# Where a norm's gain is applied: on the split weights, or on the transposed rows

## The chip, the cores and the metric

One NeuronCore of a Trainium2 chip runs the whole program in one launch. The metric is the device time of that launch in microseconds (us). The engines are TensorE (PE; PEld is its weight load), VectorE (DVE), ScalarE (ACT), GpSimd (POOL) and SyncE (SP), which issues the weights' DMAs.

## What is computed

Two transformer blocks over 256 tokens of width 1024, in float32. The first has one layer (moving-block attention and retention side by side, cross attention to a memory of 256 rows, a gated feed-forward of width 2816). The second has two layers, one with sparse attention and a short convolution, one with latent attention, each followed by a squared-ReLU feed-forward of width 4096. Every projection reads normalised rows:

```python
def _rms_norm(x, gain):
    xf = x.astype(jnp.float32)
    xf = xf * lax.rsqrt(jnp.mean(xf * xf, axis=-1, keepdims=True) + NORM_EPS)
    return xf.astype(x.dtype) * gain
...
        hn = _rms_norm(x, norm_mix_pre[layer])
...
        x = x + _rms_norm(mix, norm_mix_post[layer])
        hn = _rms_norm(x, norm_ffn_pre[layer])
        x = x + _rms_norm(_squared_relu_mlp(hn, mlp_w1[layer], mlp_w2[layer]), norm_ffn_post[layer])
```

The root of the mean square is one number a token; the gain is one number a feature, that is, one a row of the weight matrix.

## The kernel before

**Products.** The 256 tokens are two tiles (t = 0, 1) of 128 rows. A product of float32 precision is made of three float32r products (`products`, L1325): rows high x weights high, rows high x weights low, rows low x weights high. So both operands are split: high is the value rounded to float32r, low is the value minus high.

**Weights.** They come as 178 units of up to 128 x 2048 (`UNITS`, from `SCHEDULE`), by SyncE into the four slots of `w_raw`. For each unit ACT writes `w_hi` (`split`, L568) and DVE `w_lo` (`split`, L917 without a gain, L919 with one), four slots each; ACT waits until TensorE has used the slot, DVE waits until ACT has done the whole unit, TensorE waits for DVE. A unit is a triple (columns, pieces, gain column): a unit of 2048 columns holds one, two or four blocks of 128 features, and a gained unit is split in that many pieces, since the gain is a column [128, 1] of `gcol` that differs from block to block. Units without a norm in front are one piece.

**Rows.** The residual stream x is turned by TensorE in blocks of 128 x 128, four to a PSUM bank (banks 4 to 7). ACT writes a bank to `hT_hi` (`high_banks`, L587), DVE writes `hT_lo` (`low_banks`, L934), each as one instruction of 128 x 512; DVE's frees the bank, and TensorE waits for that before it reads the tile. A tile is two banks. `gT_hi`, `gT_lo` hold the memory's rows. The token's root is applied to the product when it leaves PSUM.

**The passage between two layers** (`boundary`, `boundary_after`) is written out by hand, the same on both engines. On ACT: square of tile 0 of the product, split of a unit, the high parts of tile 0 of x, square of that tile, split, square of tile 1 of the product, split, the high parts of tile 1, square. On DVE: tile 0 added to the stream (L992, L994), split, low parts of tile 0, split, tile 1 added, low parts of tile 1, split. GpSimd computes each root between the square and the addition (L462, L463). TensorE turns tile 0 before the last unit of the product's tile 1, and tile 1 beside the first product of the next layer. After mlp0 the product's rows are latents, 640 columns, split as five blocks a tile (one bank of four blocks and one of a single block). At the start the rows of x are split on ACT before the first units, and the memory's four banks are split after the third projection group.

Of the kernel before, what the change touches and what calls it, by code (L numbers as in the profile page):

```python
# [49 lines left out]
def gained(gain, count, kcs, size):  # L50

    return [(size, kcs, PRE[gain] + TURNED * j * kcs) for j in range(count)]


def plain_units(count, size=2048):
    return [(size, 1, None)] * count


def hidden_units(gain, chunks, down):
# [13 lines left out]
            ("ukv", [(2048, 2, PRE["ranks"] + 3 * TURNED)] * 2), ("odd_out", plain_units(4)),  # L73
# [28 lines left out]
def block_kernel(nc, A, out):  # L102

    with ExitStack() as ctx:
# [447 lines left out]
        def _(act):  # L552
# [38 lines left out]
            def high_rows(tile, *tiles):  # L591

                for t in tiles or range(TT):
                    high_banks(2, lambda i: (tile[:, 4 * i:4 * i + 4, t * P:(t + 1) * P], 4))
# [55 lines left out]
            def boundary(units):  # L650
# [8 lines left out]
                high_rows(hT_hi, 0)  # L659
# [5 lines left out]
                high_rows(hT_hi, 1)  # L665
                stream_square(1)

            def boundary_after(m):
# [6 lines left out]
                high_rows(hT_hi, 0)  # L675
# [5 lines left out]
                high_rows(hT_hi, 1)  # L681
# [79 lines left out]
            high_rows(hT_hi, 0)  # L761
            act.wait_ge(gcol_ready, len(PRE_ROWS))
            split_to(0)
            high_rows(hT_hi, 1)
# [38 lines left out]
            boundary(4)  # L803
# [6 lines left out]
            boundary(4)  # L810
            mlp(ffn)
            boundary_after(ffn)
# [37 lines left out]
            boundary(4)  # L850
            mlp(mlps[0])
            boundary_after(mlps[0])
# [6 lines left out]
            for t in range(TT):  # L859
# [5 lines left out]
                high_banks(2, lambda i: (hT_hi[:, 4 * i:4 + i, t * P:(t + 1) * P], 4 - 3 * i))  # L865
# [27 lines left out]
            boundary(4)  # L893
# [8 lines left out]
        def _(dve):  # L902
# [35 lines left out]
            def low_rows(hi, lo, tiles=range(TT)):  # L938
                for t in tiles:
                    low_banks(2, lambda i: (hi[:, 4 * i:4 * i + 4, t * P:(t + 1) * P], lo[:, 4 * i:4 * i + 4, t * P:(t + 1) * P], 4))  # L940
# [55 lines left out]
            def boundary(b, units, last=True):  # L996
# [7 lines left out]
                low_rows(hT_hi, hT_lo, [0])  # L1004
# [803 lines left out]
```

## Time and profile before

| what | us |
|---|---|
| median of three runs | 1137.89 (1135.34 to 1138.71) |
| profiled execution, its own time | 1135.04 |
| span of that execution, first to last instruction | 1133.2 |
| TensorE busy (matmul) | 1059.2, 93% of the span |
| DVE busy | 657.8, 58% |
| ACT busy | 563.5, 50% |
| GpSimd busy | 91.6, 8% |
| mean granted clock of TensorE | 0.981 of 2.4 GHz |

Some 2 us of the time lie outside the span. Busy times are sums over one engine's instructions; matmuls are pipelined, so their durations overlap. Times in a timeline are from the start of the span, a duration stands behind them, and in brackets is how long the engine sat idle before and what ended that.

### The profile page before, as it was taken

The numbers are of one execution on the slowest core, as the hardware profiler recorded it, in microseconds if no ns is written. First come the engines' busy times: TensorE is split into PE (matmuls) and PEld (weight loads), VectorE is DVE, ScalarE is ACT, GpSimd is POOL, SyncE is SP. The second block draws the span as 40 slices with busy tenths as digits, with TensorE's granted clock in tenths as the row PEclk, the third lists the DMA queues.
The fourth block names the chain that finished last, engine by engine and source line by source line (L and its number), as shares of the span: only waits on it lengthen the run. The fifth ranks groups of instructions, "written<-read, shape, count | busy, mean of one in ns | idle before, by whom it ended". The sixth has DMA issues, their size and how long they took to land.

```text
span 1133.2 us, 13827 instructions
## 1 busy us (share of the span) xinstructions
PE 1059.2 (93%) x5080; PEld 879.3 (78%) x5080; DVE 657.8 (58%) x1010; ACT 563.5 (50%) x855; POOL 91.6 (8%) x123
## 2 busy tenths in 40 slices
PE   6898999998999999899988899999988998999997
PEld 5687778777888888788767688888886776888886
DVE  5457565347456455647696755555564866555553
ACT  5466365336455454545444555444445645554441
POOL 1010010001000000201840100000040001000000
PEclk9899999999999999889999999999999999999999
DMA  8632145314354555454322644454244225445520
GB/s 331 255 150 112 38 171 214 155 75 144 137 218 152 190 214 185 142 186 149 140 84 75 222 168 172 180 204 160 77 136 161 76 75 223 153 182 208 187 85 37
DMA packets 28589, 176.29 MB, mean 156 GB/s; under 512 B 3440, under 2 KB 3824, under 8 KB 10112
## 3 DMA queue, kind: packets, MB, share of 16 engines
q1 hardware_dynamic: 26496, 170.08, 40.8%
q0 software_dynamic: 1296, 5.24, 1.3%
q8 instruction: 29, 0.48, 0.2%
q10 hardware_dynamic: 752, 0.36, 0.1%
q14 instruction: 16, 0.13, 0.0%
HBM read 174.62 MB, written 1.05 MB: 155 GB/s over the span
## 4 chain that ended last, share of the span: by engine, by line
PE 77%; DVE 9%; ACT 5%; issue 3%; POOL 2%; POOLq 0%; ACTq 0%; DVEq 0%
PE PS L1325 68%; PE PS L1388 3%; DVE w_lo L919 3%; ACT w_hi L568 2%; PE PS L1440 2%; PE PS L1518 2%; PE PS L1423 2%; ACT work L637 1%; DVE w_lo L917 1%; DVE h L992 1%; DVE x L994 1%; DVE work L1031 1%; POOL h L486 1%; PE PS L1431 1%; ACT hT_hi L587 1%
## 5 line engine op out<-in xcount | busy, mean ns | idle before, releaser
L919 DVE SCALAR_TENSOR_TENSOR w_lo<-w_raw,gcol,w_hi 128x512 fp32r<-128x512 f32 (+4 forms) x322 | 269.4, 894 | 218.2 <-ACT w_hi L568 218.0
L1325 PE MATMUL PS<-w_hi,hT_hi 128*128 128x512 f32 (+3 forms) x904 | 322.9, 398 | 33.0 <-DVE w_lo L919 14.7
L1325 PE MATMUL PS<-w_hi,hT_lo 128*128 128x512 f32 (+3 forms) x904 | 315.2, 390 | 0.0
L1325 PE MATMUL PS<-w_lo,hT_hi 128*128 128x512 f32 (+3 forms) x904 | 315.1, 390 | 0.0
L568 ACT ACTIVATE w_hi<-w_raw,gcol 128x512 fp32r<-128x512 f32 (+4 forms) x322 | 243.5, 824 | 99.0 <-PE PS L1325 98.8
L1325 PEld LDWEIGHTS PS<-w_hi,hT_hi 128*128 128x128 f32 x904 | 170.7, 193 | 72.4 <-issue 18.7
L1325 PEld LDWEIGHTS PS<-w_hi,hT_lo 128*128 128x128 f32 x904 | 172.4, 192 | 34.2
L1325 PEld LDWEIGHTS PS<-w_lo,hT_hi 128*128 128x128 f32 x904 | 172.7, 192 | 33.1
L917 DVE TENSOR_TENSOR w_lo<-w_raw,w_hi 128x2048 fp32r<-128x2048 f32 (+1 forms) x70 | 135.8, 1954 | 98.2 <-ACT w_hi L568 98.1
L568 ACT ACTIVATE w_hi<-w_raw 128x2048 fp32r<-128x2048 f32 (+1 forms) x70 | 114.8, 1645 | 113.1 <-PE PS L1325 113.1
L1325 PE MATMUL PS<-w_hi,gT_hi 128*128 128x512 f32 x408 | 126.8, 392 | 1.2 <-DVE w_lo L919 1.2
L1325 PE MATMUL PS<-w_hi,gT_lo 128*128 128x512 f32 x408 | 126.2, 391 | 0.0
L1325 PE MATMUL PS<-w_lo,gT_hi 128*128 128x512 f32 x408 | 126.1, 390 | 0.0
L1325 PEld LDWEIGHTS PS<-w_lo,gT_hi 128*128 128x128 f32 x408 | 76.9, 188 | 16.2
L1325 PEld LDWEIGHTS PS<-w_hi,gT_lo 128*128 128x128 f32 x408 | 76.9, 188 | 16.1
L1325 PEld LDWEIGHTS PS<-w_hi,gT_hi 128*128 128x128 f32 x408 | 76.0, 188 | 16.9 <-DVE w_lo L919 1.6
L462 POOL TENSOR_SCALAR msq<-ssq 128x1 f32<-128x1 f32 (+1 forms) x31 | 9.3, 300 | 903.1 <-ACT work L637 858.2
L623 ACT ACTIVATE arena<-PS,rstd 128x1024 f32<-128x1024 f32 (+1 forms) x24 | 25.0, 1044 | 72.4 <-PE PS L1325 55.0
L587 ACT ACTIVATE hT_hi<-PS 128x512 fp32r<-128x512 f32 (+1 forms) x46 | 25.3, 582 | 68.3 <-PE PS L1388 68.3
L992 DVE SCALAR_TENSOR_TENSOR h<-PS,rstd,gain 128x512 f32<-128x512 f32 x28 | 20.9, 747 | 45.1 <-POOL rstd L463 45.1
L934 DVE TENSOR_TENSOR hT_lo<-PS,hT_hi 128x512 fp32r<-128x512 f32 (+1 forms) x46 | 29.1, 667 | 28.6 <-ACT hT_hi L587 28.6
L1423 PE MATMUL PS<-arena 128*128 128x256 f32 (+1 forms) x160 | 36.4, 362 | 6.8 <-ACT arena L623 2.7
(145 smaller groups left out, 782.8 us busy)
## 6 DMA issues: line engine op xcount, KB each, us to landing
w_raw<-in_w SPq DMA_DIRECT2D x64, 1024.0 KB, 4.8
w_raw<-in_w_gu SPq DMA_DIRECT2D x22, 1024.0 KB, 4.8
w_raw<-in_w_in SPq DMA_DIRECT2D x11, 1024.0 KB, 7.3
w_raw<-in_w_dn SPq DMA_DIRECT2D x22, 512.0 KB, 5.2
w_raw<-in_w_out SPq DMA_DIRECT2D x4, 1024.0 KB, 4.8
w_raw<-in_w_mem_k SPq DMA_DIRECT2D x4, 1024.0 KB, 4.8
w_raw<-in_w_mem_v SPq DMA_DIRECT2D x4, 1024.0 KB, 4.8
w_raw<-in_w_cq SPq DMA_DIRECT2D x4, 1024.0 KB, 5.6
```

The source lines that it names most:

```text
L568: ins = act.activation(w_hi[:, u % RING, k * w:(k + 1) * w], w_raw[:, u % RAW, k * w:(k + 1) * w], ACT.Copy, scale=1.0 if col is None else ...
L587: act.activation(d, PS[:, 4 + n["tb"] % 4, 0:blocks * P].rearrange("p (b m) -> p b m", m=P), ACT.Copy).then_inc(tb_high, 1)
L623: ins = act.activation(dst, src, ACT.Copy, scale=scale)
L917: ins = dve.tensor_tensor(lo, raw, hi, ALU.subtract)
L919: ins = dve.scalar_tensor_tensor(out=lo, in0=raw, scalar=gcol[:, col + TURNED * k:col + TURNED * k + 1], in1=hi, op0=ALU.mult, op1=ALU.sub ...
L934: dve.tensor_tensor(lo, PS[:, 4 + n["tb"] % 4, 0:blocks * P].rearrange("p (b m) -> p b m", m=P), hi.bitcast(F32), ALU.subtract).then_inc(t ...
L992: steps.link(dve.scalar_tensor_tensor(out=h[:, t, cols], in0=PS[:, 2 * t + i, :], scalar=rstd[:, stat:stat + 1], in1=gain[:, g, cols], op0 ...
L1325: mm = pe.matmul(bank(t, j)[:, 0:width], rows[:, kc0 + k, tok], w[:, s, at:at + width], start=begin and i == 0, stop=end and i == 2)
L1388: mm = pe.transpose(PS[0:rows, 4 + n["tb"] % 4, i * P:(i + 1) * P], src, ident[:])
L1423: mm = pe.matmul(PS[:, 4 + hd % 2, c0:c1], q, k, start=i == 0, stop=i == len(pairs) - 1)
L1440: mm = pe.matmul(out_banks(a, t)[:, hd * a.dv:(hd + 1) * a.dv], a.ET[hd % 2][:, c0 + s * P:c0 + (s + 1) * P], a.v(hd, s), start=s == 0, st ...
L1518: mm = pe.transpose(m.turn_bank[t][:, b * P:(b + 1) * P], hidden[:, t, b * P:(b + 1) * P], ident[:])
```

## The change

The weights of gained units are split without their gain, in the same pieces. The gain is applied to the transposed rows instead, when these are split: ACT scales each block of 128 features by its column while it rounds, DVE multiplies and subtracts in one instruction. Since the column differs from block to block, a bank is written by four instructions on each engine instead of one; the semaphore is raised by the last of them. Rows with no norm in front (attention outputs) are still one instruction a bank. At the start ACT waits for `gcol` before the first rows. The gains reach the helpers as an argument:

```diff
 def gained(gain, count, kcs, size):
-    return [(size, kcs, PRE[gain] + TURNED * j * kcs) for j in range(count)]
+    return [(size, kcs, None)] * count
...
-            ("ukv", [(2048, 2, PRE["ranks"] + 3 * TURNED)] * 2), ("odd_out", plain_units(4)),
+            ("ukv", [(2048, 2, None)] * 2), ("odd_out", plain_units(4)),
...
-            def high_banks(count, dst):
+            def high_banks(count, dst, gain=None):
                 for i in range(count):
                     act.wait_ge(tb_ready, n["tb"] + 1)
                     d, blocks = dst(i)
+                    if gain is not None:
+                        for b in range(blocks):
+                            col = gain + TURNED * (4 * i + b)
+                            ins = act.activation(d[:, b, :], PS[:, 4 + n["tb"] % 4, b * P:(b + 1) * P], ACT.Copy, scale=gcol[:, col:col + 1])
+                        ins.then_inc(tb_high, 1)
+                        n["tb"] += 1
+                        continue
                     act.activation(d, PS[:, 4 + n["tb"] % 4, 0:blocks * P].rearrange("p (b m) -> p b m", m=P),
                                    ACT.Copy).then_inc(tb_high, 1)
...
-            high_rows(hT_hi, 0)
             act.wait_ge(gcol_ready, len(PRE_ROWS))
+            high_rows(hT_hi, 0, gain=PRE["pre_mix"])
             split_to(0)
-            high_rows(hT_hi, 1)
+            high_rows(hT_hi, 1, gain=PRE["pre_mix"])
...
-                high_rows(gT_hi)
+                high_rows(gT_hi, gain=PRE["mem"])
...
-            def low_banks(count, dst):
+            def low_banks(count, dst, gain=None):
...
+                    if gain is not None:
+                        for b in range(blocks):
+                            col = gain + TURNED * (4 * i + b)
+                            ins = dve.scalar_tensor_tensor(out=lo[:, b, :], in0=PS[:, 4 + n["tb"] % 4, b * P:(b + 1) * P],
+                                                           scalar=gcol[:, col:col + 1], in1=hi[:, b, :].bitcast(F32),
+                                                           op0=ALU.mult, op1=ALU.subtract)
+                        ins.then_inc(tb_free[n["tb"] % 4], 1)
+                        n["tb"] += 1
+                        continue
                     dve.tensor_tensor(lo, PS[:, 4 + n["tb"] % 4, 0:blocks * P].rearrange("p (b m) -> p b m", m=P),
                                       hi.bitcast(F32), ALU.subtract).then_inc(tb_free[n["tb"] % 4], 1)
...
-                low_rows(hT_hi, hT_lo, [0])
+                low_rows(hT_hi, hT_lo, [0], gain)
...
-            boundary(5, 4)
+            boundary(5, 4, PRE["ffn_pre1"])
```

All six passages, the start, the memory's rows and the latents' rows are changed alike: 36 banks, two of which hold one block.

The next two extracts are ACT's instructions in the passage before the first feed-forward layer, first before, then changed (`work,ssq` is a square; the line numbers move because of the new code):

```order
L637 ACTIVATE work,ssq<-PS 128x1024
L568 ACTIVATE w_hi<-w_raw,gcol 128x512 x8
L587 ACTIVATE hT_hi<-PS 128x4x128 x2
L637 ACTIVATE work,ssq<-x 128x1024
L568 ACTIVATE w_hi<-w_raw,gcol 128x512 x4
L637 ACTIVATE work,ssq<-PS 128x1024
L568 ACTIVATE w_hi<-w_raw,gcol 128x512 x4
L587 ACTIVATE hT_hi<-PS 128x4x128 x2
L637 ACTIVATE work,ssq<-x 128x1024
```

```order
L644 ACTIVATE work,ssq<-PS 128x1024
L568 ACTIVATE w_hi<-w_raw 128x512 x8
L590 ACTIVATE hT_hi<-PS,gcol 128x128 x8
L644 ACTIVATE work,ssq<-x 128x1024
L568 ACTIVATE w_hi<-w_raw 128x512 x4
L644 ACTIVATE work,ssq<-PS 128x1024
L568 ACTIVATE w_hi<-w_raw 128x512 x4
L590 ACTIVATE hT_hi<-PS,gcol 128x128 x8
L644 ACTIVATE work,ssq<-x 128x1024
```

No instruction changed its place; the splits lose `gcol` and keep their four pieces a unit, and a tile's rows are eight instructions instead of two. The same on DVE, in the passage after that layer, before and changed:

```order
L992 SCALAR_TENSOR_TENSOR h<-PS,rstd,gain 128x512
L994 TENSOR_TENSOR x<-x,h 128x512
L919 SCALAR_TENSOR_TENSOR w_lo<-w_raw,gcol,w_hi 128x1024 x2
L934 TENSOR_TENSOR hT_lo<-PS,hT_hi 128x4x128 x2
L919 SCALAR_TENSOR_TENSOR w_lo<-w_raw,gcol,w_hi 128x1024 x2
```

```order
L1008 SCALAR_TENSOR_TENSOR h<-PS,rstd,gain 128x512
L1010 TENSOR_TENSOR x<-x,h 128x512
L924 TENSOR_TENSOR w_lo<-w_raw,w_hi 128x1024 x2
L944 SCALAR_TENSOR_TENSOR hT_lo<-PS,gcol,hT_hi 128x128 x8
L924 TENSOR_TENSOR w_lo<-w_raw,w_hi 128x1024 x2
```

Here too the order stays, the weights' operation becomes a plain subtraction, and the rows' becomes eight multiply-subtracts.

## Rows read from the trace of the kernel before

**Rows 1.** The waits, all engines: who waited for whom: us in total, times, longest.

```profile
PE PS L1325 <- DVE w_lo L919: 15.9, 9, 4.8
PE PS L1325 <- DVE hT_lo L934: 10.5, 8, 1.6
```

**Rows 2.** Groups by shape: line, operation, shapes, count | busy us, mean ns | idle before.

```profile
L568 ACT ACTIVATE w_hi<-w_raw,gcol 128x1024 fp32r<-128x1024 f32 x84 | 91.3, 1142 | 18.3 <-PE PS L1325 18.2
L568 ACT ACTIVATE w_hi<-w_raw 128x1024 fp32r<-128x1024 f32 x22 | 23.3, 1057 | 22.9 <-PE PS L1325 22.9
L919 DVE SCALAR_TENSOR_TENSOR w_lo<-w_raw,gcol,w_hi 128x512 fp32r<-128x512 f32 x216 | 147.9, 747 | 125.9 <-ACT w_hi L568 125.9
L934 DVE TENSOR_TENSOR hT_lo<-PS,hT_hi 128x512 fp32r<-128x512 f32 x44 | 28.7, 685 | 28.6 <-ACT hT_hi L587 28.6
```

**Rows 3.** Small pieces: groups, then timeline (start us, us, instructions).

```profile
L623 ACT ACTIVATE h<-PS,rstd 128x64 f32<-128x64 f32 x4 | 1.0, 310 | 3.6 <-PE PS L1325 3.6
L714 ACT ACTIVATE arena<-PS,rstd 128x256 f32<-128x256 f32 x22 | 10.3, 474 | 25.3 <-PE PS L1325 25.3
489.36 0.51 ACT L623 ACTIVATE h<-PS,rstd 128x64 f32<-128x64 f32 x2
280.78 0.84 ACT L714 ACTIVATE arena<-PS,rstd 128x256 f32<-128x256 f32 x2
480.33 1.79 DVE L919 SCALAR_TENSOR_TENSOR w_lo<-w_raw,gcol,w_hi 128x80 fp32r<-128x80 f32 x8 [6.20 <-ACT w_hi L568]
281.29 0.88 DVE L1069 SCALAR_TENSOR_TENSOR arena<-PS,rstd,arena 128x256 f32<-128x256 f32 x2 [0.56 <-ACT arena L714]
```

**Rows 4.** Timeline of the passage before the first feed-forward layer, ACT, DVE and PE.

```profile
261.42 1.09 ACT L587 ACTIVATE hT_hi<-PS 128x512 fp32r<-128x512 f32 x2 [0.53 <-PE PS L1388]
263.57 1.28 DVE L934 TENSOR_TENSOR hT_lo<-PS,hT_hi 128x512 fp32r<-128x512 f32 x2
268.68 0.74 DVE L992 SCALAR_TENSOR_TENSOR h<-PS,rstd,gain 128x512 f32<-128x512 f32 x1
271.59 0.66 PE L1388 MATMUL PS<-ident,x 128*128 128x128 f32 x4 [0.50 <-DVE x L994]
272.28 0.60 ACT L587 ACTIVATE hT_hi<-PS 128x512 fp32r<-128x512 f32 x1 [0.56 <-PE PS L1388]
273.75 0.47 PE L1325 MATMUL PS<-w_hi,hT_hi 128*128 128x512 f32 x1 [1.50 <-DVE hT_lo L934]
```

**Rows 5.** Timeline of PE, the start: first waits for w_lo.

```profile
20.38 0.73 PE L1325 MATMUL PS<-w_hi,hT_hi 128*128 128x512 f32 x2 [1.84 <-DVE w_lo L919]
43.38 1.19 PE L1325 MATMUL PS<-w_hi,hT_hi 128*128 128x512 f32 x2 [4.77 <-DVE w_lo L919]
```

**Rows 6.** Timeline, memory rows on ACT and the wait behind them.

```profile
90.18 2.07 ACT L587 ACTIVATE gT_hi<-PS 128x512 fp32r<-128x512 f32 x4 [3.90 <-PE PS L1388]
96.89 3.39 PE L1423 MATMUL PS<-arena 128*128 128x128 f32 x10 [2.71 <-ACT arena L623]
```

**Rows 7.** Timeline of PE, memory keys and first product of the sparse layer.

```profile
156.63 0.74 PE L1325 MATMUL PS<-w_hi,gT_hi 128*128 128x512 f32 x2 [1.17 <-DVE w_lo L919]
461.63 1.19 PE L1325 MATMUL PS<-w_hi,hT_hi 128*128 128x512 f32 x2 [0.63 <-DVE hT_lo L934]
```

**Rows 8.** Timeline, the latents' second tile on ACT and PE's wait.

```profile
841.97 0.77 ACT L587 ACTIVATE hT_hi<-PS 128x512 fp32r<-128x512 f32 x2 [3.04 <-PE PS L1388]
843.64 0.59 PE L1325 MATMUL PS<-w_hi,hT_hi 128*128 128x384 f32 x2 [1.59 <-DVE hT_lo L934]
```

**Rows 9.** Timeline of DVE beside GpSimd's index sum.

```profile
552.96 7.21 DVE L919 SCALAR_TENSOR_TENSOR w_lo<-w_raw,gcol,w_hi 128x1024 fp32r<-128x1024 f32 x4 [6.45 <-ACT w_hi L568]
```

**Rows 10.** The chain that ended last: start us, us, what; a stretch in a loop.

```profile
316.22 16.37 PE PS L1325 x72
```

**Rows 11.** Timeline of PE after the wait at 273.75, first and last of seven.

```profile
274.43 0.63 PE L1325 MATMUL PS<-w_hi,hT_lo 128*128 128x512 f32 x1
276.99 0.63 PE L1325 MATMUL PS<-w_hi,hT_lo 128*128 128x512 f32 x1
```

More of the change, by code:

```diff
@@ L589, in high_banks, with high_rows @@
                     n["tb"] += 1
-            def high_rows(tile, *tiles):
+            def high_rows(tile, *tiles, gain=None):
                 for t in tiles or range(TT):
-                    high_banks(2, lambda i: (tile[:, 4 * i:4 * i + 4, t * P:(t + 1) * P], 4))
+                    high_banks(2, lambda i: (tile[:, 4 * i:4 * i + 4, t * P:(t + 1) * P], 4), gain)
             def plain_banks(count, dst, parity=0):
@@ L648, in half_rows, with boundary @@
                 return lambda i: (tile[:, chunk:chunk + 4, token_cols(i)], 4)
-            def boundary(units):
+            def boundary(units, gain):
                 split_to(n["used"] + 3)
@@ L658, in boundary @@
                 split_to(e + 1)
-                high_rows(hT_hi, 0)
+                high_rows(hT_hi, 0, gain=gain)
                 stream_square(0)
@@ L674, in boundary_after @@
                 split_to(e + 1)
-                high_rows(hT_hi, 0)
+                high_rows(hT_hi, 0, gain=gain)
                 stream_square(0)
@@ L680, in boundary_after @@
                 split_to(e + 3)
-                high_rows(hT_hi, 1)
+                high_rows(hT_hi, 1, gain=gain)
                 stream_square(1)
@@ L802, in _ @@
             act.wait_ge(ret_ss, TT)
-            boundary(4)
+            boundary(4, PRE["pre_cross"])
             group(4, rows2(k_tok), mem_rows)
@@ L809, in _ @@
             high_rows(hT_hi)
-            boundary(4)
+            boundary(4, PRE["pre_ffn"])
             mlp(ffn)
-            boundary_after(ffn)
+            boundary_after(ffn, PRE["mix_pre0"])
             def even_rows(t):
@@ L892, in _ @@
             high_rows(hT_hi)
-            boundary(4)
+            boundary(4, PRE["ffn_pre1"])
             mlp(mlps[1])
@@ L994, in add_to_stream, with boundary @@
                     dve.tensor_tensor(x[:, t, cols], x[:, t, cols], h[:, t, cols], ALU.add).then_inc(x_ready, 1)
-            def boundary(b, units, last=True):
+            def boundary(b, units, gain, last=True):
                 split_to(n["used"] + 3)
@@ L1008, in boundary, with boundary_after @@
                     split_to(e + 3)
-                low_rows(hT_hi, hT_lo, [1])
+                low_rows(hT_hi, hT_lo, [1], gain)
                 split_to(e + 3)
-            def boundary_after(b, m):
+            def boundary_after(b, m, gain):
                 e = m_end(m)
@@ L1016, in boundary_after @@
                 split_to(e + 1)
-                low_rows(hT_hi, hT_lo, [0])
+                low_rows(hT_hi, hT_lo, [0], gain)
                 split_to(e + 2)
@@ L1020, in boundary_after @@
                 split_to(e + 3)
-                low_rows(hT_hi, hT_lo, [1])
+                low_rows(hT_hi, hT_lo, [1], gain)
             def attention(a):
@@ L1127, in half_rows @@
                 return lambda i: (hT_hi[:, chunk:chunk + 4, token_cols(i)], hT_lo[:, chunk:chunk + 4, token_cols(i)], 4)
-            low_rows(hT_hi, hT_lo, [0])
+            low_rows(hT_hi, hT_lo, [0], PRE["pre_mix"])
             split_to(0)
-            low_rows(hT_hi, hT_lo, [1])
+            low_rows(hT_hi, hT_lo, [1], PRE["pre_mix"])
             split_to(1)
@@ L1179, in _ @@
             low_banks(2, half_rows(4))
-            boundary(0, 4, False)
+            boundary(0, 4, PRE["pre_cross"], False)
             after_group(4)
@@ L1276, in _ @@
                 split_to(e + 2 * t)
-                low_banks(2, lambda i: (hT_hi[:, 4 * i:4 + i, t * P:(t + 1) * P], hT_lo[:, 4 * i:4 + i, t * P:(t + 1) * P], 4 - 3 * i))
+                low_banks(2, lambda i: (hT_hi[:, 4 * i:4 + i, t * P:(t + 1) * P], hT_lo[:, 4 * i:4 + i, t * P:(t + 1) * P], 4 - 3 * i), PRE["ranks"])
                 split_to(e + 1 + t)
```

25 lines of the change are left out of this document (12 added, 13 removed).

## The prediction

> **What bounds the kernel now.** I read three views, in this order: the waits by engine, the instruction groups with shapes kept apart, and the order of time around each place where the matmuls stop. TensorE is busy for most of the span, so an edit on ScalarE (ACT) or VectorE (DVE) counts only where TensorE waits for it. In the loops of the feed-forward layers it never waits long for weights; what is left are the passages between two layers. There the rows of the residual stream are turned, split by ACT into hT_hi and by DVE into hT_lo, and only then can the next products start. TensorE waits 8 times, 10.5 us in all, for hT_lo and 9 times, 15.9 us, for the gained w_lo [rows 1]. So the question is which of the two splits ends last at each passage, since the change makes one of them dearer and the other cheaper.
>
> **Price of the weights' splits.** The factor is a pointer operand. The change drops it and, as the order shows, keeps the pieces: a unit is still two pieces of 1024 or four of 512. On ACT a 1024 piece takes 1142 ns with the pointer and 1057 without; on DVE 512 columns cost 747 ns as scalar_tensor_tensor (the add at the boundary, L992, has the same shape) and 685 as tensor_tensor [rows 2]. I take 0.09 us a piece off ACT and 0.06 off DVE: a unit of two gives 0.18 and 0.12, a unit of four 0.35 and 0.25. Over 322 pieces that is 29 and 19 us of busy time, nearly all beside running matmuls.
>
> **Price of the rows' splits.** A bank of 512 columns becomes four pieces of 128, each with its own factor. No such piece is in the trace. On ACT, from PSUM with a pointer, two pieces of 64 take 0.51 us together and two of 256 take 0.84; with 310 and 474 ns for one, the starts lie 0.20 and 0.37 apart [rows 3]. These are the two ends; 128 lies a third of the way, 0.26. A tile of eight pieces then takes 7 x 0.26 + 0.36 = 2.15 us, where two pieces of 512 take 1.09 [rows 4]: **+1.05 us a tile**, and the first bank is done after 1.12 instead of 0.60. On DVE eight pieces of 80 take 1.79 us, starts some 0.21 apart, and two of 256 from PSUM 0.88, starts some 0.40 apart [rows 3]; for 128 I take 0.27: eight need 2.2 us instead of 1.28 [rows 4], **+0.9**, four 1.15 instead of 0.69.
>
> The Trainium skill, ScalarE: Activation LUTs, section "What ACT_TABLE_LOAD costs", gives 186 ns + 0.833 ns a column, about 93 ns more for a pointer and about 93 ns of overlap. By that an estimate for 128 columns is 0.29 us from start to start, 2.4 us a tile, and the sum below would be some 2.5 us higher; our PSUM rows at 64 and 256 columns lie below it, and they decide.
>
> **The passages**, each by what ends last:
> - Start. Both tiles' rows stand on ACT in front of the squares and the split of unit 2, for which TensorE waits 1.84 us [rows 5]. The first tile ends 0.7 later (ACT used to wait inside it for TensorE), the second adds 1.05; units 0 to 2 give back 0.35 on ACT and 0.12 on DVE: +1.3. The wait in front of the next group (4.77 us [rows 5]) ends on a split by ACT and one by DVE and is 0.3 shorter. Net **+1.0**.
> - Memory rows. Four banks on ACT take 2.07 us [rows 6]; sixteen pieces take 15 x 0.26 + 0.36 = 4.26. Behind them on ACT stand two plain splits and the copy that TensorE waits 2.71 us for [rows 6]. DVE follows at the same distance. **+2.2**.
> - Before the memory keys. The tile's rows push ACT's second square back by 1.05 - 0.18; GpSimd's root, DVE's add and the split that TensorE waits for [rows 7] follow, 0.12 shorter: **+0.75**.
> - Before a feed-forward layer, three times the same pattern (the rows shown are the first). Tile 0: DVE's two splits are 0.5 shorter, then its rows 0.9 longer, so TensorE starts 0.35 later, which the second tile covers. ACT then is 1.05 - 0.35 = 0.7 late with the second square; so are the root, the add at 268.68 and the last transpose. Its bank takes ACT 0.5 and DVE 0.45 longer, and TensorE, which stood from 272.25 to 273.75 for just that bank [rows 4], starts 1.6 later. Three times: **+4.8**.
> - After the first feed-forward layer. DVE: -0.12 +0.9 on the tile that TensorE waits 0.63 for [rows 7]; the second tile has about 0.5 of slack and needs 0.8: **+1.1**.
> - After mlp0, down to the latents. Tile 0 +0.3, second square and add +1.2 (0.1 of it given back), tile 1 +0.3 more; then the latents' tiles, five pieces of 128, 4 x 0.26 + 0.36 = 1.4 against 0.77 on ACT and 0.3 more on DVE, on which the 1.59 us wait at 843.64 ends [rows 8]: **+2.45**.
> - Sparse attention. Here only the weights' splits stand in the chain to GpSimd's index sum: -0.16, -0.27, and for the four pieces that take DVE 7.21 us beside GpSimd [rows 9] -0.4: **-0.85**. The latents' last projection: **-0.3**.
>
> Sum: 1.0 + 2.2 + 0.75 + 4.8 + 1.1 + 2.45 - 0.85 - 0.3 = **+11.1 us**. In the loops the change is worth nothing, because 72 matmuls run there without a gap, 0.23 us apart [rows 10]; were that cover gone, two gained units an iteration, 1.2 us, would show.
>
> **The clock.** After a long stop TensorE is granted 1.2 GHz for a while: behind the 1.5 us wait at 273.75, matmuls start 0.43 us apart from 274.43 to 276.99 [rows 11] where the loop has 0.23; some eight matmuls at 0.2 extra make 1.6 us. Most stops that get longer have such a stretch already; the one before the last feed-forward layer, the latents' and the one before the memory keys have none. I count two more: **+3.2**. Together +14.3 on the profiled execution's 1135.0, so 1149.3; that execution stands 2.9 below the median 1137.9 of three runs, from which it would be 1152.2. I predict **1151**, between the two; the rivals are reckoned from 1138.
>
> The Trainium skill, VectorE: DVE Perf Modes, section "The TRN2 errata — SBUF-src ops pay a fixed extra latency per instruction", speaks against this change: it says small tiles pay the fixed part each time and advises tiles of at least 512 elements. The rows agree in kind: eight pieces of 80 columns, 640 in all, take DVE 1.79 us, more than twice one piece of 512 [rows 2, 3].
>
> **Rivals.**
> 1. Pieces are cheap or half hidden. With ACT starts 0.20 apart, the lower bound, a tile costs 0.45 less, and where root or transpose ends last it costs nothing: about half of the rows' terms go, +5, **1143**. For it: the 64-column row. Against: in the passage shown [rows 4] nothing stands between ACT's row piece and TensorE's start.
> 2. Slower pieces or a lost clock. Starts 0.30 apart add about 3, low stretches at five further stops instead of two add 5: the sum is then +17 or +19, **1157**. For it: stops of 3 us arise at four places.
> 3. Faster: what ends last at the passages is the weights' split, and a row piece costs its columns alone. From the sum, a tile's cost vanishes where ACT's starts are about 0.14 apart; below 0.16 the givebacks of 0.3 to 0.6 a passage win: -4, **1134**. Against: 64 columns already need 0.20.
> 4. No change: the factor's cost moves from one cover to another, and the waits are set by the root and the transposes: **1138**. A form of it is that the change does not do what it says: that the pieces without pointer cost the same as before. That alone would raise my sum by some 4.
>
> **How the numbers follow.** Forecast 0.62, rival 1 0.16, rival 2 0.12, rival 4 0.07, rival 3 0.03. Slower by over 0.3% (3.4 us, about what a measurement here can tell from no change) is the sum of the first three, 0.90; the same 0.07; faster 0.03. The bounds of the ACT piece (0.20 to 0.37) alone would give +5 to +22; the upper end needs 256 columns' price for 128, so I stop at 1158 and at 1142, with rivals 1 and 2 inside.
>
> **What would show it.** Right: ACT's busy time falls by some 29 us for the weights and rises by about 12 for the rows, pieces start 0.26 apart; TensorE's waits for hT_lo grow from 10.5 to about 20 us; the loops keep their length; matmul count and pitch are unchanged. Wrong: waits for hT_lo stay near 10 us, or TensorE's new waits name w_lo or the transposes, or the loss lies inside the loops.

## The result and the profile after

The changed kernel takes **1148.72 us** (median of four runs, 1147.1 to 1148.92), the kernel before, timed beside it, 1138.07 (1135.34 to 1138.71): ratio 1.0095, 95% interval 1.0076 to 1.0114. It is slower by about 10.7 us, and the forecast was 1151, 1142 to 1158. The profiled execution took 1148.6 us; its span, 1146.7 us, is 13.5 longer than the one before.

The page's first part shows TensorE 4 us busier, ACT 10 less and DVE 4 less; the number of matmuls is the same.

```profile
span 1146.7 us, 14031 instructions
PE 1063.4 (93%) x5080; PEld 881.6 (77%) x5080; DVE 653.9 (57%) x1112; ACT 553.5 (48%) x957; POOL 93.2 (8%) x123
```

The waits of the changed kernel, which answer to [rows 1] (who waited for whom: us in total, times, longest):

```profile
PE PS L1341 <- DVE w_lo L924: 15.1, 10, 4.5
PE PS L1341 <- DVE hT_lo L944: 13.7, 9, 2.6
PE PS L1341 <- DVE hT_lo L950: 4.0, 4, 1.6
```

L944 writes rows with a gain, L950 rows without one. Together the waits for hT_lo rose from 10.5 to 17.7 us, while the wait for w_lo hardly moved. If every row in this view that has PE on its left is added, TensorE's stops are 65.8 us before and 75.3 after: +9.5 of the 13.5. Of these, 7.2 name hT_lo and 2.1 the copy behind the memory's rows.

The groups by shape, which answer to [rows 2] and give the pieces that no trace had shown:

```profile
L924 DVE TENSOR_TENSOR w_lo<-w_raw,w_hi 128x512 fp32r<-128x512 f32 x216 | 134.9, 686 | 113.3 <-ACT w_hi L568 113.3
L568 ACT ACTIVATE w_hi<-w_raw 128x512 fp32r<-128x512 f32 x216 | 118.5, 627 | 75.7 <-PE PS L1341 75.7
L568 ACT ACTIVATE w_hi<-w_raw 128x1024 fp32r<-128x1024 f32 x106 | 107.2, 1058 | 45.6 <-PE PS L1341 45.6
L590 ACT ACTIVATE hT_hi<-PS,gcol 128x128 fp32r<-128x128 f32 x122 | 33.7, 382 | 39.9 <-PE PS L1404 39.9
L944 DVE SCALAR_TENSOR_TENSOR hT_lo<-PS,gcol,hT_hi 128x128 fp32r<-128x128 f32 x122 | 33.2, 343 | 28.9 <-ACT hT_hi L590 28.9
```

A plain piece costs what was forecast (1058 ns on ACT, 686 on DVE). A row piece takes ACT 382 ns alone; in the timeline below eight take 2.17 us, so their starts lie (2.17 - 0.38) / 7 = 0.256 us apart.

The timeline of the passage before the first feed-forward layer, the counterpart of [rows 4]:

```profile
264.13 2.17 ACT L590 ACTIVATE hT_hi<-PS,gcol 128x128 fp32r<-128x128 f32 x8 [0.91 <-PE PS L1404]
265.67 2.15 DVE L944 SCALAR_TENSOR_TENSOR hT_lo<-PS,gcol,hT_hi 128x128 fp32r<-128x128 f32 x8
271.86 0.74 DVE L1008 SCALAR_TENSOR_TENSOR h<-PS,rstd,gain 128x512 f32<-128x512 f32 x1
274.78 0.66 PE L1404 MATMUL PS<-ident,x 128*128 128x128 f32 x4 [0.69 <-DVE x L1010]
275.47 1.14 ACT L590 ACTIVATE hT_hi<-PS,gcol 128x128 fp32r<-128x128 f32 x4 [0.21 <-PE PS L1404]
276.64 1.13 DVE L944 SCALAR_TENSOR_TENSOR hT_lo<-PS,gcol,hT_hi 128x128 fp32r<-128x128 f32 x4 [0.22 <-ACT hT_hi L590]
277.92 0.70 PE L1341 MATMUL PS<-w_hi,hT_hi 128*128 128x512 f32 x1 [2.48 <-DVE hT_lo L944]
```

Nothing else stands between the last transpose and TensorE's start: four pieces on ACT, four on DVE, and the 1.50 us stop has become 2.48. The same number stands before the second and the third feed-forward layer (1.50 before, 2.48 after, both times). With the smaller stops beside it, each of the three passages has 1.3 to 1.4 us more of stops, 4.1 together.

The other places, from the timeline of TensorE and ACT ([rows 5 to 8] in that order):

```profile
21.67 0.73 PE L1341 MATMUL PS<-w_hi,hT_hi 128*128 128x512 f32 x2 [1.70 <-DVE w_lo L924]
42.77 1.19 PE L1341 MATMUL PS<-w_hi,hT_hi 128*128 128x512 f32 x2 [4.46 <-DVE w_lo L924]
88.47 4.23 ACT L590 ACTIVATE gT_hi<-PS,gcol 128x128 fp32r<-128x128 f32 x16 [3.88 <-PE PS L1404]
97.35 2.93 PE L1439 MATMUL PS<-arena 128*128 128x128 f32 x8 [4.85 <-ACT arena L630]
157.78 0.73 PE L1341 MATMUL PS<-w_hi,gT_hi 128*128 128x512 f32 x2 [1.83 <-DVE w_lo L924]
466.29 1.19 PE L1341 MATMUL PS<-w_hi,hT_hi 128*128 128x512 f32 x2 [1.35 <-DVE hT_lo L944]
846.12 0.59 PE L1341 MATMUL PS<-w_hi,hT_hi 128*128 128x384 f32 x2 [0.93 <-DVE hT_lo L944]
850.36 1.40 ACT L590 ACTIVATE hT_hi<-PS,gcol 128x128 fp32r<-128x128 f32 x5 [3.07 <-PE PS L1404]
853.07 0.59 PE L1341 MATMUL PS<-w_hi,hT_hi 128*128 128x384 f32 x2 [2.63 <-DVE hT_lo L944]
```

The stops are longer where a term stood for it: 2.71 to 4.85 behind the memory's rows, 1.17 to 1.83 before the memory keys, 0.63 to 1.35 after the first feed-forward layer, 1.59 to 2.63 at the second tile of the latents. The first two, in the start, are shorter (1.84 to 1.70 and 4.77 to 4.46).

One of the new stops costs nothing against the kernel before: 1.31 us at 871.27, behind the latents' last projection. In the kernel before, the clock was low there (from 857.8), and TensorE was so slow that it had nothing to wait for: from its start behind the stop to the transposes it took 4.44 us, now 4.31.

```profile
857.89 1.19 PE L1325 MATMUL PS<-w_hi,hT_hi 128*128 128x512 f32 x2 [2.84 <-DVE w_lo L919]
862.33 1.95 PE L1388 MATMUL PS<-ident,h 128*96 128x128 f32 x16
866.96 0.70 PE L1341 MATMUL PS<-w_hi,hT_hi 128*128 128x512 f32 x2 [2.53 <-DVE w_lo L924]
871.27 1.95 PE L1404 MATMUL PS<-ident,h 128*96 128x128 f32 x16 [1.31 <-DVE h L995]
```

The first two lines are of the kernel before. So stops and low clock are not two separate accounts: a low stretch can hide a stop.

In the loop nothing moved; the chain that ended last, against [rows 10]:

```profile
320.44 16.37 PE PS L1341 x72
```

The rest of the 13.5 us goes with the clock. The stretches table (start and end, length, busy times of the engines with their counts, then the granted clock) shows full speed up to the stop at 157.78 and half of it right behind, where the kernel before had none, and again in the sparse attention:

```profile
150.00:158.00 8.00, 6.17 (x28) 4.81 (x27) 7.21 (x8) 2.65 (x4) 1.63 (x2) 1.00 0.36 132
158.50:161.90 3.40, 3.40 (x10) 2.65 (x9) 0.00 (x0) 0.00 (x0) 0.00 (x0) 0.50 0.86 308
592.00:599.00 7.00, 6.50 (x28) 5.34 (x27) 5.36 (x16) 3.49 (x15) 5.79 (x3) 0.51 0.00 0
```

Ahead of the program's tail (its last 4 to 7 us, at low clock in every profile), the granted clock was 1.2 instead of 2.4 GHz for 40.8 us before and for 51.0 after. The part of the span that is not a stop grew by 4.0 (1067.4 to 1071.4), so by this pair of executions a microsecond of low clock costs about 0.4. A line through the nine profiles below without added matmuls gives 0.41; the second profile of the changed kernel lies 2.8 us off it, so a single pair can't bear this alone.

### The profile page after: what moved, and what is told of

Its sections match the earlier page's. It is cut to its first block, busy times and chain, and to the rows that moved or that the text cites. A ratio compares the mean times of both kernels' runs of the same rounds, so it can differ in the third digit from the quotient of the medians.

```text
span 1146.7 us, 14031 instructions
## 1 busy us (share of the span) xinstructions
PE 1063.4 (93%) x5080; PEld 881.6 (77%) x5080; DVE 653.9 (57%) x1112; ACT 553.5 (48%) x957; POOL 93.2 (8%) x123
## 3 DMA queue, kind: packets, MB, share of 16 engines
HBM read 174.62 MB, written 1.05 MB: 153 GB/s over the span
## 4 chain that ended last, share of the span: by engine, by line
PE 79%; DVE 9%; ACT 6%; issue 2%; POOL 1%; POOLq 0%; ACTq 0%; DVEq 0%
PE PS L1341 68%; DVE w_lo L924 4%; PE PS L1404 3%; ACT w_hi L568 2%; PE PS L1456 2%; PE PS L1439 2%; PE PS L1534 2%; ACT hT_hi L590 1%; PE PS L1675 1%; DVE hT_lo L944 1%; DVE h L1008 1%; DVE x L1010 1%; ACT work L644 1%; PE PS L1447 1%; DVE work L1047 1%
## 5 line engine op out<-in xcount | busy, mean ns | idle before, releaser
L924 DVE TENSOR_TENSOR w_lo<-w_raw,w_hi 128x512 fp32r<-128x512 f32 (+5 forms) x392 | 386.0, 1035 | 313.4 <-ACT w_hi L568 313.3
L568 ACT ACTIVATE w_hi<-w_raw 128x512 fp32r<-128x512 f32 (+5 forms) x392 | 329.4, 901 | 227.9 <-PE PS L1341 227.8
L1341 PE MATMUL PS<-w_hi,hT_hi 128*128 128x512 f32 (+3 forms) x904 | 322.5, 398 | 38.8 <-DVE hT_lo L944 13.7
L1341 PEld LDWEIGHTS PS<-w_hi,gT_hi 128*128 128x128 f32 x408 | 76.4, 189 | 17.7 <-DVE w_lo L924 2.3
L462 POOL TENSOR_SCALAR msq<-ssq 128x1 f32<-128x1 f32 (+1 forms) x31 | 9.2, 298 | 923.7 <-ACT work L644 876.3
L590 ACT ACTIVATE hT_hi<-PS,gcol 128x128 fp32r<-128x128 f32 x122 | 33.7, 382 | 39.9 <-PE PS L1404 39.9
L944 DVE SCALAR_TENSOR_TENSOR hT_lo<-PS,gcol,hT_hi 128x128 fp32r<-128x128 f32 x122 | 33.2, 343 | 28.9 <-ACT hT_hi L590 28.9
L1439 PE MATMUL PS<-arena 128*128 128x256 f32 (+1 forms) x160 | 39.0, 381 | 10.0 <-ACT arena L630 4.9
L701 ACT ACTIVATE work<-work,attention_bias 128x128 f32<-128x128 f32 x64 | 28.5, 446 | 25.1 <-DVE attention_bias L1054 25.0
L1095 DVE TENSOR_TENSOR gT_lo<-PS,gT_hi 128x512 fp32r<-128x512 f32 (+1 forms) x54 | 28.8, 575 | 18.5 <-ACT gT_hi L729 18.5
```

Source lines behind the costliest of these rows:

```text
L568: ins = act.activation(w_hi[:, u % RING, k * w:(k + 1) * w], w_raw[:, u % RAW, k * w:(k + 1) * w], ACT.Copy, scale=1.0 if col is None else ...
L590: ins = act.activation(d[:, b, :], PS[:, 4 + n["tb"] % 4, b * P:(b + 1) * P], ACT.Copy, scale=gcol[:, col:col + 1])
L701: ins = act.activation(a.E[hd % 3][:, c0:c1], src, ACT.Exp, bias=a.nb[:, hd, t:t + 1], scale=a.scale, accum_out=a.sums[:, hd, t:t + 1])
L924: ins = dve.tensor_tensor(lo, raw, hi, ALU.subtract)
L944: ins = dve.scalar_tensor_tensor(out=lo[:, b, :], in0=PS[:, 4 + n["tb"] % 4, b * P:(b + 1) * P], scalar=gcol[:, col:col + 1], in1=hi[:, b, ...
L1095: dve.tensor_tensor(m.rows_of(gT_lo, c, t), m.turn_bank[t][:, 0:m.cols].rearrange("p (b m) -> p b m", m=P), m.rows_of(gT_hi, c, t).bitcast ...
```

## Experiments

All runs stand against the kernel before, timed on the same chip beside them. "Stops" is the sum over TensorE's waits in the profiled execution, "low" its time at 1.2 GHz ahead of the tail, "clock" the mean granted clock, median over all runs of the kernel (for the kernel before 0.981 or 0.982, by chip). The kernels share helpers that take a list of norms for each side; the extracts show what those lists come to.

The last column takes the clock out. The kernel before ran 23 times beside the first kernels: 1129.95 us to 1138.61, at clocks from 0.985 to 0.976. Time follows the clock there on a line of 7.4 us for each 0.01 (7.0 to 7.6 on the four chips), and none of the 83 runs is more than 2 us off its line. "Equal clock" is a kernel's mean time less what the line of its chip gives for the kernel's mean clock. Clocks above 0.990 lie beyond the runs of the kernel before, so for the "busy" kernels the line is extended.

| kernel | ratio (95%) | stops | low | clock | equal clock, us |
|---|---|---|---|---|---|
| before | 1 | 65.8 | 40.8 | 0.981 | 0 |
| changed | 1.0095 (1.0076 to 1.0114) | 75.3 | 51.0 | 0.976 | not known |
| changed, again | 1.0101 (1.0072 to 1.0130) | 74.9 | 37.4 | 0.979 | +10.7 |
| weights plain only | 0.9958 (0.9941 to 0.9976) | 62.0 | 40.9 | 0.980 | -5.5 |
| rows and weights | 1.0165 (1.0136 to 1.0194) | 77.1 | 44.2 | 0.975 | +12.8 |
| one piece | 1.0149 (1.0120 to 1.0177) | 73.6 | 61.2 | 0.971 | +10.8 |
| two blocks a piece | 1.0040 (1.0016 to 1.0064) | 65.3 | 47.6 | 0.975 | +0.8 |
| feed-forward on weights | 1.0055 (1.0032 to 1.0078) | 68.5 | 57.9 | 0.978 | +4.4 |
| sparse rows | 0.9983 (0.9961 to 1.0006) | 65.3 | 40.8 | 0.981 | -0.1 |
| busy before | 0.9898 (0.9873 to 0.9924) | 47.9 | 3.4 | 0.997 | +1.5 |
| busy before, again | 0.9904 (0.9869 to 0.9939) | 47.8 | 10.2 | 0.997 | +0.7 |
| busy after | 1.0011 (0.9988 to 1.0034) | 54.7 | 6.8 | 0.989 | +8.9 |
| busy sparse | 0.9970 (0.9947 to 0.9993) | 49.2 | 13.6 | 0.988 | +0.9 |
| busy sparse, early | 0.9934 (0.9909 to 0.9959) | 44.4 | 20.5 | 0.990 | -0.8 |

### The two halves of the change

**Weights plain only**: the gains left out on both sides.

```diff
 def gained(gain, count, kcs, size):
-    return [(size, kcs, PRE[gain] + TURNED * j * kcs) for j in range(count)]
+    return [(size, kcs, None)] * count
```

> This is one half of the change alone: the weights are split without their gain and the rows are split as before, so the gains in front of the projections are left out of the computation. Theory A (the row pieces lengthen the passages, the weights' splits give a little back): time falls against the kernel before by what the cheaper splits are worth where TensorE waits for them, 3 to 5 us (ratio 0.996 to 0.997), and TensorE's waits for hT_lo stay near 10 us. Theory B (the change is mainly one of the clock's low stretches): no more than 1 us either way.

Measured: 1129.55 against 1133.8, 4.3 us faster; stops 3.8 us shorter, the clock nearly as before (0.980 to 0.982), as expected. **Rows and weights**: the rows' half on top of the old weights, so the gain is applied twice.

```diff
-                low_rows(hT_hi, hT_lo, [0])
+                low_rows(hT_hi, hT_lo, [0], gain)
...
 def gained(gain, count, kcs, size):
     return [(size, kcs, PRE[gain] + TURNED * j * kcs) for j in range(count)]
```

> The other half alone: the rows are split in gained pieces of 128 columns, and the weights keep their gains too, so each gain is applied twice. Theory A: slower than the kernel before by the rows' terms of the sum without the give-back, some 14 us plus or minus 3 (ratio 1.010 to 1.015), and slower than the changed kernel by 3 to 5 us. Theory B: within 2 us of the changed kernel's loss, with the difference to before found in the count of low stretches of the clock.

Measured: 1151.45, 17.7 us slower, a little over the 1.010 to 1.015 expected; stops +11.3, and a lower clock (0.975). The rows' half (+1.65%) less the weights' half (0.42%) is 1.23%, against 0.95% for the whole change; the gap of 0.28 is within the three intervals together. What the change does to the weights is worth something; what it does to the rows costs about four times as much.

### Does the number of pieces cost it?

**Two blocks a piece**: a bank's rows in two instructions of 256 columns, on both engines; every second block is scaled by its neighbour's column.

```diff
-                        for b in range(blocks):
+                        for b in range(0, blocks, 2):
+                            e = min(b + 2, blocks)
                             col = gain + TURNED * (4 * i + b)
...
-                            ins = act.activation(d[:, b, :], PS[:, 4 + n["tb"] % 4, b * P:(b + 1) * P], ACT.Copy, scale=gcol[:, col:col + 1])
+                            ins = act.activation(d[:, b:e, :], PS[:, 4 + n["tb"] % 4, b * P:e * P].rearrange("p (b m) -> p b m", m=P),
+                                                 ACT.Copy, scale=gcol[:, col:col + 1])
```

> The changed kernel, but a bank's rows are written in two instructions of 256 columns on each engine instead of four of 128; the second block of each pair is scaled by the first one's column, so half of the gains are left out of the computation. My theory: the loss is the start-to-start cost of the row pieces. By the 256-column row of the kernel before (0.84 us for two, starts 0.37 apart) a tile of four takes ACT 3 x 0.37 + 0.47 = 1.6 us, 0.55 to 0.6 less than eight of 128 (2.17) and 0.5 more than two of 512. So about half of the rows' part of the loss goes: TensorE's stops fall from 75 to about 69 us, and the time is 1.004 to 1.007 of before (4 to 8 us over it). A rival, that scaling by a pointer or the multiply on VectorE is what costs and not the number of pieces: the stops stay at 75 and the time at 1.009 to 1.010. Another, that any extra piece is enough to shift the clock's low stretches: stops 69, but 1.009 too.

Measured: 1.0040, stops 65.3. The timeline of the same passage in this kernel:

```profile
271.61 0.84 ACT L602 ACTIVATE hT_hi<-PS,gcol 128x256 fp32r<-128x256 f32 x2 [0.39 <-PE PS L1418]
272.49 0.87 DVE L958 SCALAR_TENSOR_TENSOR hT_lo<-PS,gcol,hT_hi 128x256 fp32r<-128x256 f32 x2 [0.35 <-ACT hT_hi L602]
273.51 0.77 PE L1355 MATMUL PS<-w_hi,hT_hi 128*128 128x512 f32 x1 [1.93 <-DVE hT_lo L958]
```

Half the pieces, and the stop stands at 1.93, near the middle between 1.50 and 2.48: the length of this stop goes with the number of pieces, and the pointer and the multiplication, which stayed, are at most a part of what it costs. The stops fell further than the 69 us expected, back to the level of before; part of that is a low stretch at 13.9 which hides all but 0.39 of the stop that is 1.70 long in the changed kernel. The time lies at the lower edge of what was expected. It is still 0.4% above before, at equal stops, with a clock of 0.975 instead of 0.982, and at equal clock only 0.8 us above. So here the low clock is nearly all that is left. That is the second rival's mechanism, at a smaller price than the rival gave it. Why half the pieces leave so little of the 10.7 us at equal clock, less than their pitch explains, stays open.

**One piece**: the changed kernel, with each unit's split, now plain, in one instruction of the full 2048 columns instead of two or four.

```diff
 def gained(gain, count, kcs, size):
-    return [(size, kcs, None)] * count
+    return [(size, 1, None)] * count
```

> The changed kernel with each gained unit split in one instruction on ACT and one on DVE instead of one, two, four or eight. Theory A: a unit of four pieces is then 0.27 us shorter on ACT and 0.2 on DVE, a unit of two 0.1 and 0.1; in the passages this gives back 0.2 to 0.5 us each, 2 to 3 us in all against the changed kernel (ratio to the kernel before 1.006 to 1.008). Theory B: same as the changed kernel, 1.009.

Measured: 1.0149, half a per cent slower than the changed kernel where I expected it faster: a miss. The stops are in fact 1.7 us shorter and ACT is busy for 19 us less, but the low clock rose to 61.2 us. GpSimd shows one thing that long pieces do. In this kernel's timeline GpSimd's operation on a square's sum, one column, lasts as long as the whole split beside it; in the changed kernel (the last two lines, the same place) it ends with the first of four pieces:

```profile
276.32 2.28 DVE L935 TENSOR_TENSOR w_lo<-w_raw,w_hi 128x2048 fp32r<-128x2048 f32 x1
276.37 2.28 POOL L473 TENSOR_SCALAR msq<-ssq 128x1 f32<-128x1 f32 x1 [5.91 <-ACT work L655]
277.69 2.49 DVE L924 TENSOR_TENSOR w_lo<-w_raw,w_hi 128x512 fp32r<-128x512 f32 x4
277.73 0.68 POOL L462 TENSOR_SCALAR msq<-ssq 128x1 f32<-128x1 f32 x1 [5.98 <-ACT work L644]
```

Over the kernel the groups give that operation a mean of 660 ns, and the changed kernel 302 (group L462):

```profile
L473 POOL TENSOR_SCALAR msq<-ssq 128x1 f32<-128x1 f32 x30 | 19.8, 660 | 873.2 <-ACT work L655 872.9
```

The Trainium skill, SBUF — State Buffer, section "Who interferes with whom", says that a DVE instruction with two inputs from SBUF contends with a GpSimd instruction that reads SBUF. The first two rows above agree: the short operation ends within 0.05 us of the long one. What made the kernel slower is the clock: at equal clock it is 10.8 us above before, as the changed kernel is (10.7). That GpSimd's longer operations, rather than some other shift of the stops, moved the clock's stretches was not shown.

### Which passages?

**Feed-forward on weights**: the changed kernel with the three norms before the feed-forward layers back on the weights.

```diff
-            boundary(4, PRE["pre_ffn"])
+            boundary(4)
...
-            boundary(4, PRE["ffn_pre0"])
+            boundary(4)
...
-            boundary(5, 4, PRE["ffn_pre1"])
+            boundary(5, 4)
```

> The changed kernel with the gains of the three norms in front of feed-forward layers back on the weights, and their six tiles of rows in two pieces again. Theory A: each of the three passages is shorter by 1.5 us against the changed kernel and the loops keep their length, so -4.5 us, and up to 3 us more where the shorter stops no longer bring a low stretch of the clock: ratio to the kernel before 1.003 to 1.006. TensorE's wait for the second tile in these passages is 1.5 us again instead of 2.5. Theory B: a change below 1.5 us, unless low stretches vanish.

Measured: 1.0055, as expected; stops 6.8 us shorter than in the changed kernel. The stop in front of the second tile is 1.50 or 1.51 us again in all three passages, and the passages have 4.1 us less of stops, just what they had gained. Most of the other 2.7 us lies in the start and behind the memory's rows, whose gains this kernel still has on the rows; there, low stretches at 14.6 and 96.6 stand next to the shorter stops.

**Sparse rows**: the kernel before, with only the norm in front of sparse attention on its rows, the one layer for which the forecast had a gain to set against its loss (+1.1 at the entrance, -0.85 at the index sum).

```diff
-            boundary_after(ffn)
+            boundary_after(ffn, PRE["mix_pre0"])
```

> Only the norm in front of the sparse attention layer has its gain on the rows; the other eight stay on the weights. By the terms found in the two traces the passage costs 1.1 us and the plain splits in front of the index sum give back 1.3. Theory A: TensorE's stops within 0.5 us of the kernel before, time the same within 0.3% (ratio 0.997 to 1.003). Rival: the give-back belongs to all the splits before the sparse layer together, then ratio 1.001 to 1.004, slower.

Measured: 0.9983, not to be told from no change (0.9961 to 1.0006); stops 65.3 against 65.8. Loss and gain do cancel, to within what is measured here. **The changed kernel again**, on that chip:

> The changed kernel once more, beside the same runs of the kernel before as the next three, with a second profile. Theory A (TensorE's stops grow by some 9.5 us, the rest of the loss is where the clock's low stretches fall): TensorE's stops add up to 75 us again, within 1, and the granted clock's low stretches lie elsewhere than in the first profile, their sum differing by 3 us or more; ratio 1.008 to 1.013. Theory B (the low stretches belong to the program): the same stretches at the same places within 1 us.

Measured: 1.0101, the first ratio within its interval. Its low clock is 37.4 us in the profiled execution, where the first showed 51.0, at nearly the same stops: where the stretches fall is not a property of the kernel alone. Beside each other on that chip, the mean clock of all runs is 0.978 against 0.980, worth 1.1 us, and at equal clock the change costs 10.7 us. So the loss is nearly all in the stops, and the clock's share in the first profile, 4 us, is more than the change costs there on average.

### The clock held up

**Busy before** and **busy after**: small matmuls of the identity with the mask, 96 of them, into a free bank, placed in TensorE's stops in front of the semaphores it waits for; nothing reads their result. The extract shows one of the places.

```diff
+            def keep_busy(count, bank):
+                pe.wait_ge(const_loaded, 64)
+                for _ in range(count):
+                    pe.matmul(PS[:, bank, 0:256], ident[:], causal[:], start=True, stop=True)
...
+                        if busy and j == 0 and t == 0:
+                            keep_busy(busy, 0)
                         if t == 0:
                             split_ready(n["u"] + j)
```

> The kernel before with the same matmuls at the same places. Theory A: five to seven of its ten low stretches vanish, ratio 0.990 to 0.996, and the changed kernel with them is slower than this one by its longer stops alone, 9 to 10 us less what the matmuls cost where they overrun a stop. Theory B: ratio 1.000 to 1.003.

> The changed kernel with small matmuls that nobody reads (128x256, the identity by the mask) at nine kinds of places where TensorE stops for more than 1 us: the start, the memory rows, the passages into the feed-forward layers, the end of the first feed-forward layer and of the latent attention. Theory A (the stops bring the low stretches, and the clock's share of the loss is theirs): most of the low stretches behind these places vanish, 8 to 11 of the 13 shown, which is worth 1.5 us each; the time falls by 5 to 12 us, to a ratio of 0.998 to 1.005. Theory B (the low stretches have another cause): their number stays, and the time rises by 0 to 3 us, 1.010 to 1.013.

Measured: the kernel before becomes 1.0% **faster**, 1124.37 against 1135.51, a hair under the 0.990 to 0.996 expected and the lowest ratio of all; the changed kernel with the same matmuls is at 1.0011. Their groups row, in the kernel before:

```profile
L1364 PE MATMUL PS<-causal,ident 128*128 128x256 f32 x96 | 22.7, 379 | 0.0
```

The clock's median is 0.997 instead of 0.981. At equal clock this kernel is 1.5 us slower than before, so it is the clock that wins, and the added matmuls themselves cost a little. With the same matmuls the changed kernel is 13.3 us behind (1137.65 to 1124.37), more than without them and more than the 9 to 10 expected: a miss. The stops differ by 6.8 us; the clock differs by 0.0075, 5.7 us at 7.6 for each 0.01. So with the clock held up the change costs its stops, and it also costs part of the clock that the filling had won. The numbers of matmuls are the same in both, against longer stops in the changed kernel; that this is why, was not shown here.

**Busy sparse**: busy before, with the sparse layer's gain on the rows, the edit that had cost nothing. **Busy before, again**, beside it.

```diff
-            boundary_after(ffn)
+            boundary_after(ffn, PRE["mix_pre0"])
```

> The kernel before with both edits that did not lose: small unused matmuls in TensorE's stops, and the gain in front of sparse attention on the rows. Theory: the matmuls keep the clock at 2.4 GHz (0.9898 by themselves), and with the clock held what is left of the rows' edit is its effect on the stops, which lengthened by 1.1 us in front of the sparse layer and shortened by about 1.3 us at GpSimd's index sum. So 0.988 to 0.991, no different from the matmuls alone by more than 1.5 us. Rival: the index sum's gain (the chain to GpSimd) was hidden by the clock and shows fully: 0.986 to 0.988.

> The kernel before with the unused matmuls in the stops, once more, for comparison on the same chip as the other two. Theory: the gain comes from the clock and from nothing that differs between chips: 0.988 to 0.992, mean granted clock 0.995 or more, under 7 us of low stretches before the tail. Rival, that the first measurement caught a favourable placement of the stretches: 0.993 or above.

Measured: busy before 0.9904, as the first time, though with 10.2 us of low clock in its profile where under 7 were expected; busy sparse 0.9970 where at most 0.991 was expected, a miss. The stops differ by 1.4 us and the medians by 6.6; at equal clock the two are alike (+0.9 and +0.7), so what was lost is clock. Timeline and stretches of busy before, first execution:

```profile
458.12 0.70 PE L1352 MATMUL PS<-w_hi,hT_hi 128*128 128x512 f32 x2 [1.75 <-DVE hT_lo L961]
457.40:460.80 3.40, 2.68 (x12) 2.23 (x13) 2.50 (x3) 3.40 (x6) 1.06 (x3) 1.00 0.90 308
484.80:491.60 6.80, 6.80 (x38) 5.89 (x38) 6.53 (x11) 2.82 (x6) 0.00 (x0) 1.00 0.78 304
```

and of busy sparse:

```profile
456.01 0.70 PE L1352 MATMUL PS<-w_hi,hT_hi 128*128 128x512 f32 x2 [2.49 <-DVE hT_lo L955]
457.40:460.80 3.40, 3.40 (x10) 2.66 (x9) 2.92 (x5) 1.72 (x2) 1.54 (x2) 0.51 0.42 125
484.80:491.60 6.80, 6.80 (x25) 6.03 (x24) 4.95 (x9) 2.58 (x6) 0.00 (x0) 0.50 0.75 289
```

The stop for the rows is 2.49 us instead of 1.75, and behind the longer one the clock is low. Busy after, feed-forward on weights and the changed kernel, again, have the same stop at 2.50 us and a low stretch behind it too; busy before, again, has 1.75 and none. The second stretch is another matter. In busy sparse 25 matmuls ran in it instead of 38, but busy before, again, has a low stretch there as well, behind the shorter stop:

```profile
457.40:460.80 3.40, 2.73 (x12) 2.31 (x13) 2.50 (x3) 3.40 (x6) 1.06 (x3) 1.00 0.85 308
484.10:490.90 6.80, 6.80 (x27) 6.26 (x28) 4.58 (x8) 3.23 (x9) 0.00 (x0) 0.51 0.86 325
```

So the longer stop goes with the first stretch, and the second can't be put down to it.

**Busy sparse, early**: four more of these matmuls in that very stop.

```diff
+                            if early and t == 0:
+                                keep_busy(early, 0)
                             if rows is not None:
...
-            project(4, 2, wide, copies=2, rows=rows, hooks={(0, 3): tile1})
+            project(4, 2, wide, copies=2, rows=rows, early=4, hooks={(0, 3): tile1})
```

> The kernel with matmuls in the stops and the gain in front of sparse attention on the rows, plus four more unused matmuls in the stop in front of that layer (2.49 us at 456.01 in its profile, against 1.75 without the rows' edit, where no low stretch followed). Theory: the longer stop itself brings the low clock behind it (457.4 in that profile), and that is most of what separates 0.997 from 0.990. Then the stop shrinks to under 1 us, the stretch behind it is gone, the mean granted clock is 0.992 or more, and the time is 0.989 to 0.993 of before. Rival: what was lost does not lie there but later in the layer (the low stretches at 484.8 and 576.9 of that profile), whatever is done to this stop: 0.995 to 0.998, with clocks of 0.987 to 0.991.

Measured: 0.9934, between the two expectations. The stop and the stretch behind it are gone, and two of nine runs reach a clock of 0.995 and 1123.37 to 1124.93 us, the level of busy before; the other seven stay at 0.990, and in the profiled one the low clock stands at 451.6, 485.8 and, for 13.7 us, 574.5 instead. So this stop is part of the cause at most, and where the rest of the low clock comes from is open.

## Why the prediction was right

The direction, the size and the mechanism came out as forecast; 1148.7 lies 2.3 us under the number. That the total is so close is partly luck: in the profiled execution the stops came out 1.6 us under their sum and the clock 0.8 over its term. By its steps:

- **Price of the weights' splits**: 1058 and 686 ns, as taken.
- **Price of the rows' splits**: ACT starts 0.256 us apart where 0.26 was interpolated, a tile 2.17 us for 2.15; DVE 2.15 for 2.2. The estimate of 0.29 from the Trainium skill, ScalarE: Activation LUTs, section "What ACT_TABLE_LOAD costs", was too high, and the neighbouring rows in PSUM decided rightly.
- **The passages**, in us by TensorE's stops and starts at matched places: start +0.7 (forecast +1.0), memory rows +2.1 (+2.2), before the memory keys +0.7 (+0.75), first feed-forward passage +1.4 (+1.6) and the three together +4.1 (+4.8), after the first feed-forward layer +1.1 (+1.1), latents +2.0 (+2.45), last projection of the latents -0.3 (-0.3), sparse attention about -1.0 (-0.85). The stops in total: **+9.5 where the sum said +11.1**, and 1.3 of the 9.5 is the stop at 871.27 that cost nothing. The overshoot is in the feed-forward passages, the start and the latents. A reading that no run tests: both the longer rows and the later squares were counted in full there, though part of one lay beside the other.
- **Sparse attention** gave back what was forecast. From the transposes behind the stop at 511.43 (514.58 in the changed kernel) to those at 580.73 (583.04), with 320 matmuls between them in both, it takes 69.30 us before and 68.46 after, 0.84 less; the stop at 511.43 is 0.2 shorter.
- **The clock**: +4.0 for the +3.2 taken. That is right as a size for this execution, and luck in part: on the second chip the clock was worth 1.1 us on average. The step behind it, that two certain stops get a stretch each, was too definite. Of the three places named, the one before the memory keys (158.5) and the last feed-forward layer (957.2 and 967.5) did get one and the latents did not; but stretches at 21.5 and 857.8 went away, two came in sparse attention (585.1 and 592.0, 10.2 us together), and the second execution had less low clock than the kernel before.
- **ACT's busy time** fell by 10 us, not by 29 - 12 = 17. The rows' side was mis-added: 34 full banks are 17 tiles at 1.05 us, 18 us. It changed nothing, as ACT's sum bounds nothing.
- **Waits for hT_lo** reached 17.7 us, not "about 20".

**Rival 1** (cheap pieces) fell with the pitch of 0.256; **rival 3** with the halves measured apart: the weights' split alone brings only 4.3 us. **Rival 2** is right in kind, as the two-block kernel shows a loss of clock with no longer stops, and wrong in size: ACT's starts were not 0.30 apart, and low clock rose by 10.2 us in one profile of the changed kernel and fell by 3.4 in the other. **Rival 4** holds for one layer, sparse attention, and not for the kernel.

## What to carry over

Before a factor is moved from a large operand to a small one, ask at which moment each is processed: here the weights' splits lie beside running matmuls for nearly all of their 322 pieces, while the 138 row pieces lie in the few passages in which TensorE stops for them. In such a passage the price of cutting one instruction in four is the pitch of the small pieces, and here it was well interpolated from rows with the same source and operand form at nearby sizes. A stop costs its length and sometimes also the clock behind it, so an edit that loses nothing on one version can lose on another whose clock is better kept, and small matmuls in the stops (0.990 here) are worth trying before any of it. Since the clock alone spreads the runs of one kernel over 9 to 12 us here, compare kernels over many runs and at equal clock before a few microseconds are put down to an edit.

## What was not expected of the hardware

- Matmuls that nobody reads, 22.7 us of them in stops, raise the mean granted clock from 0.981 to 0.997 and make the kernel 1% faster.
- Two executions of the same program, with stops of 75.3 and 74.9 us, had 51.0 and 37.4 us of low clock; the runs of the kernel before lie on a line of time against clock, 7.0 to 7.6 us for each 0.01, within 2 us.
- A GpSimd operation on one column took 2.28 us beside a DVE subtraction of 2048 columns that reads both inputs from SBUF, and 0.68 us in the changed kernel at the same place.
